# Depthwise convolution of a diffusion backbone on VectorE: one instruction a tap, or two in turn

## The reference, cut to what matters

```
CONV_WIDTH = 31
D_CONV = 512

def dwconv(x, w):
    '''Centred depthwise convolution over positions, zero padded. x (B,T,C), w (W,C).'''
    return lax.conv_general_dilated(x, w[:, None, :], window_strides=(1,), padding='SAME', ...)

def conv_module(glu_in, dw_w, ln_g, ln_b):
    a, b = jnp.split(glu_in, 2, axis=-1)
    u = a * jax.nn.sigmoid(b)
    u = dwconv(u, dw_w)
    u = layer_norm(u, ln_g, ln_b)
    return jax.nn.silu(u)
```

## Time and profile before

| | us |
|---|---|
| median of 3 runs | 1950.89 (1950.55 to 1960.35) |
| span of the profiled execution, first to last instruction | 1948.7 |
| median over that span, what lies around it | 2.2 |
| PE busy | 1757.5 (90%) |
| DVE busy | 1201.7 (62%) |
| POOL busy | 611.3 (31%) |
| ACT busy | 557.4 (29%) |
| share of L1414 in the chain that ended last | 8% |

### The profile page before, as it was taken

One profiled execution on the slowest core, in us unless ns is written; L12 is line 12 of the kernel. 1 busy time (PEld: TensorE's weight loads), 2 busy tenths in 40 slices (PEclk: granted clock), 3 DMA queues, 4 the chain that ended last, 5 costly groups with the idle time before them and its releaser, 6 DMA issues.

```text
span 1948.7 us, 25524 instructions
## 1 busy us (share of the span) xinstructions
PE 1757.5 (90%) x9480; PEld 1495.6 (77%) x9480; DVE 1201.7 (62%) x1757; ACT 557.4 (29%) x777; POOL 611.3 (31%) x282
## 2 busy tenths in 40 slices
PE   5799994777978999999999999798899899999997
PEld 4688883555877888888888888677677778888885
DVE  8888987455877888676853872742683544153243
ACT  1323122553223232122211222231232343223232
POOL 2433330221332343223432323241002245444441
PEclk8699996799988999999999999798899899999998
DMA  8232210002421334333332322031001023332221
GB/s 286 65 80 74 65 44 33 17 17 79 145 80 44 117 100 139 119 96 120 97 119 87 97 86 76 1 111 44 1 1 56 31 87 97 97 98 96 86 92 60
DMA packets 156400, 157.71 MB, mean 81 GB/s; under 512 B 9442, under 2 KB 153506, under 8 KB 156330
## 3 DMA queue, kind: packets, MB, share of 16 engines
q1 hardware_dynamic: 156330, 156.77, 25.1%
HBM read 154.63 MB, written 2.12 MB: 80 GB/s over the span
## 4 chain that ended last, share of the span: by engine, by line
PE 58%; DVE 25%; issue 9%; ACT 3%; DMA 2%; POOL 1%; DVEq 1%; SPq 1%; ACTq 0%; POOLq 0%
PE acc L479 45%; DVE conv_u L1414 8%; DVE ada_acc L1229 4%; PE acc L492 2%; PE acc L822 2%; DVE hid L1585 2%; PE acc L665 2%; DVE xT L1313 2%; DVE ada_acc_b L1229 1%; PE acc L801 1%; PE acc L505 1%; DMA ada_w<-in_ada_w 1%; DVE y L1210 1%; PE acc L776 1%; PE acc L514 1%
## 5 line engine op out<-in xcount | busy, mean ns | idle before, releaser
L1754 POOL TENSOR_TENSOR w_lo<-raw,w_hi 128x1024 fp32r<-128x1024 f32 x190 | 519.7, 2756 | 1033.7 <-ACT w_hi L848 1033.7
L479 PE MATMUL acc<-h_hi,w_hi 128*128 128x512 f32 x1744 | 520.3, 357 | 15.1 <-DVE h_lo L1288 4.4
L479 PE MATMUL acc<-h_lo,w_hi 128*128 128x512 f32 x1744 | 516.4, 355 | 0.0
L479 PE MATMUL acc<-h_hi,w_lo 128*128 128x512 f32 x1744 | 515.7, 355 | 0.0
L479 PEld LDWEIGHTS acc<-h_hi,w_hi 128*128 128x128 f32 x1744 | 287.2, 191 | 66.2 <-DVE h_lo L1288 4.3
L479 PEld LDWEIGHTS acc<-h_lo,w_hi 128*128 128x128 f32 x1744 | 287.0, 191 | 47.2
L479 PEld LDWEIGHTS acc<-h_hi,w_lo 128*128 128x128 f32 x1744 | 286.7, 190 | 47.6
L1229 DVE SCALAR_TENSOR_TENSOR ada_acc<-ada_w,cond,ada_acc 128x256 f32<-128x256 f32 x476 | 278.2, 655 | 1.6
L848 ACT ACTIVATE w_hi<-raw 128x1024 fp32r<-128x1024 f32 x190 | 193.9, 1054 | 219.9 <-PE acc L479 96.8
L1414 DVE SCALAR_TENSOR_TENSOR conv_u<-conv_u,dw_w x120 | 158.5, 1321 | 21.7 <-DVE conv_u L1414 21.0
L479 PE MATMUL acc<-hid_hi,w_hi 128*128 128x512 f32 (+1 forms) x528 | 160.7, 359 | 0.0
(11 more groups left out here) (214 smaller groups left out, 1788.4 us busy)
## 6 DMA issues: line engine op xcount, KB each, us to landing
raw<-in_ffn_w_in SPq DMA_DIRECT2D x88, 512.0 KB, 3.5
ada_w<-in_ada_w SPq DMA_DIRECT2D x80, 512.0 KB, 3.6
raw<-in_ffn_w_out SPq DMA_DIRECT2D x40, 512.0 KB, 3.4
raw<-in_even_w_in SPq DMA_DIRECT2D x24, 512.0 KB, 3.6
ada<-in_ada_w SPq DMA_DIRECT2D x8, 1024.0 KB, 11.8
raw<-in_odd_w_in SPq DMA_DIRECT2D x12, 512.0 KB, 3.4
raw<-in_even_w_out SPq DMA_DIRECT2D x8, 512.0 KB, 4.7
raw<-in_odd_w_out SPq DMA_DIRECT2D x8, 512.0 KB, 3.4
```

The costliest lines, as they stand in the source:

```text
L479: last = nc.tensor.matmul(acc[:, s, m, t0:t1], w[:, slot, kk, c], x[:, k, t0:t1], start=(k == 0 and q == 0), stop=(k == ktiles - 1 and q = ...
L1754: nc.gpsimd.tensor_tensor(w_lo[:, n % 4], raw[:, n % 2], w_hi[:, n % 4].bitcast(F32), ALU.subtract).then_inc(low, 1)
```

## The change

Each tap becomes two instructions, one over the 512 latent columns and one over the 256 context columns, in turn. Each waits for the last instruction but one, which is the one that it adds to; the 15 columns between are no longer computed. Tap 0's two don't wait for each other. The wait for everything before stands once, ahead of a tile's first tap.

```diff
-            taps_len = LAT + HALF + CTX
+            taps = ((HALF, LAT), (U_CTX, CTX))
...
                 with dve.Fori(0, 2) as t:
-                    sd.loop(t, TAPS)
-                    dst = conv_u[:, bass.ds(t + first, 1), HALF:HALF + taps_len]
+                    sd.loop(t, 2 * TAPS)
+                    sd.wait()
                     for w in range(TAPS):
-                        src = conv_u[:, bass.ds(t + (first + 1), 1), w:w + taps_len]
-
-                        sd.wait()
                         tap = dw_w[:, w, bass.ds(t + first, 1)]
-                        if w == 0:
-                            ins = nc.vector.tensor_scalar(dst, src, tap, None, ALU.mult)
-                        else:
-                            ins = nc.vector.scalar_tensor_tensor(dst, src, tap, dst, ALU.mult, ALU.add)
-                        sd.done(ins)
+                        for c, n in taps:
+                            dst = conv_u[:, bass.ds(t + first, 1), c:c + n]
+                            src = conv_u[:, bass.ds(t + (first + 1), 1), c - HALF + w:c - HALF + w + n]
+                            if w == 0:
+                                ins = nc.vector.tensor_scalar(dst, src, tap, None, ALU.mult)
+                            else:
+                                sd.wait(sd.value() - 1)
+                                ins = nc.vector.scalar_tensor_tensor(dst, src, tap, dst, ALU.mult, ALU.add)
+                            sd.done(ins)
                     sd.end(2)
                 sd.wait()
```

## The result

The change makes the kernel about 1% slower: 1970.24 us, the median of 4 runs (1964.3 to 1978.81), beside 1950.72 for the kernel before. The ratio is 1.0096, with a 95% interval of 1.0049 to 1.0143. Forecast were 1996 us. The direction was right and the size was not: 19.5 us came and 45 were forecast. The number that came out is the one of the rival "one window more", 1971.5.

A forecast was written before the change was run, and what follows sets the result against it. DVE's stretch to 329.5 was taken to set L643, PE's 22.1 us behind it. PE's waits for w_lo move L643 from 329.7 to 375, clock terms cancel: 1950.9 + 45 = 1996 us; own range 1982 to 2012, 8 in 10 1935 to 2006.

The forecast's parts named there:

- one window more: Rival, chance 0.24: POOL still gets in at 2.8 us in tiles 1 and 3; L643 at 350, +20.6 us, 1971.5.
- The price of a tap: Convolution on DVE: two overlapping pieces cost 1.06 us a tap against 1.215, 18.6 us saved; added queue work costs nothing.
- POOL's w_lo beside a back-to-back stream: 18 w_lo instructions on the taps cost 2.14 us each back to back against 1.88, 4.7 us lost in all.
- the sum's marker at 315: conv_done, the marker behind the convolution, comes at 315 if w_lo keeps its 5.5 us pairs.
- That POOL is shut out, and that this decides: Convolution: unbroken 32.5 us streams keep POOL from w_lo, PE waits, and L643 starts 45 us later.
- The first pair's wait: Tile 0: the gate unit's w_lo pair, asked for at 138.1, is done at 164.5; PE starts at 162.1.
- POOL gets in during about the first 2.4 us of a back-to-back stream: Beside DVE's streams: POOL enters w_lo during about the first 2.4 us, after that only at a stop.
- POOL asks at about 167.3 ... 2.8 us old: too late: Tile 1: POOL's request misses the stream; w_lo done at 199, PE waits 29 us, qkov 0 is 38.4 us late.
- The clock: L643 may be shorter by 3 us behind busy units, against 3 us for PE's last restart: they cancel.
- POOL as before: Sum if POOL is served as now: -14.2 us, 1937 us, or 1929 if L643 returns to full clock.
- It stays as it was for POOL: Rival, chance 0.27: POOL slips in at piece boundaries even late in a stream, PE isn't delayed; 1937 or 1929 us.
- Nothing gained by overlap: Rival, chance 0.07 with gains that cancel: pieces end to end, 1.03 + 0.2 us a tap, within 2 us of now.

The follow-up runs named there:

- run 4: The changed kernel, with POOL writing zeros by memset to w_lo for the last 20 granules beside the convolution: 1919.52 us, ratio 0.9838.
- run 8: The kernel before, with POOL writing zeros by memset to w_lo for the last 20 granules beside the convolution: 1922.17 us, ratio 0.987.
- run 2: The changed kernel, but at every 4th tap the 512-column piece waits for the last instruction, a stop of DVE: 1939.63 us, ratio 0.9958.
- run 3: The changed kernel, but at every 8th tap the 512-column piece waits for the last instruction, a stop of DVE: 1933.55 us, ratio 0.992.
- run 6: The changed kernel, with a one-column DVE memset (a door) before every 4th tap and no added wait: 1935.18 us, ratio 0.9937.
- run 7: The changed kernel, with one stop of DVE a tile, at tap 16: 1929.11 us, ratio 0.9914.
- run 11: The changed kernel, with a one-column DVE memset (a door) before every 8th tap and no added wait: 1934.6 us, ratio 0.9923.
- run 5: The changed kernel once more, unaltered, to see its spread: 1971.29 us, ratio 1.0103.
- run 9: The changed kernel, but each tap is three pieces of 256 columns, each waiting for the last instruction but two: 2021.41 us, ratio 1.0378.
- run 1: The changed kernel, but the 512-column piece of every tap waits for the last instruction, a stop a tap: 1971.22 us, ratio 1.010.

## Why the prediction was right and where it was wrong

- **The price of a tap: right.** Forecast 1.06 us and nothing for the queue's added work; measured 31.87 us for sixty pieces, and 19.05 us between runs 4 and 8 for 18.9. Every piece of the four tiles started 0.66 or 0.40 us after the one before, where POOL wasn't in between.
- **POOL's w_lo beside a back-to-back stream, 2.14 us instead of 1.88: right.** Four taps with one take 6.47 us against 4.33 in run 2. With POOL served as before, the sum's marker at 315 stands beside 316.85, 315.90 and 315.26 (a stop every 8th tap, a door every 4th and every 8th).
- **That POOL is shut out, and that this decides: right.** Runs 2, 3, 6, 7 and 11 each open the stream now and then, change nothing else, and all are faster than the kernel before.
- **The first pair's wait: right.** Forecast from 138.1 to 164.5, measured 136.92 to 163.34; PE held back until 160.97 (forecast 162.1).
- **The step that failed: "POOL gets in during about the first 2.4 us of a back-to-back stream", and with it "POOL asks at about 167.3 ... 2.8 us old: too late".** POOL asked at 165.84, 2.50 us behind its last entry, and was let in at the boundary 2.85 us behind it. The same came again at 260.30. The prediction measured in time, on an FFN stream that opens with four short tap-0 pieces. Counted, the request that missed there at 964.08 came in the seventh instruction of its stream, where it goes both ways, and the one here in the sixth (fifth, if the piece that had waited for POOL isn't counted). So one pair more got in within tile 1 and one within tile 2, PE was spared the 29 us wait before qkov 0, and L643 began 24.4 us later instead of 45. The trace of before already spoke against an edge of 2.4 us. There POOL asked at 986.23, 3.4 us into a back-to-back stream of DVE's whose first instruction is long, in its sixth instruction, and got in (POOL, then DVE):

```profile
986.23 5.28 POOL L1754 TENSOR_TENSOR w_lo<-raw,w_hi 128x1024 fp32r<-128x1024 f32 x2 [11.36 <-ACT w_hi L848]
```
```profile
982.84 1.76 DVE L1210 TENSOR_TENSOR hid_lo<-hid,hid_hi  x1 [1.73 <-ACT hid_hi L1096]
984.52 0.61 DVE L1222 TENSOR_SCALAR ada_acc<-ada_w,cond 128x256 f32<-128x256 f32 x2
985.04 7.26 DVE L1229 SCALAR_TENSOR_TENSOR ada_acc<-ada_w,cond,ada_acc 128x256 f32<-128x256 f32 x7
```

- **The entry in mid-stream was not foreseen.** POOL had asked at 241.16 and was let in at 252.91, beside the 48th of tile 2's sixty pieces. There the queue's row (REGISTER_ALU) came 0.05 us ahead of its 256-column piece, where it elsewhere comes 0.4 us ahead of one. In run 5 the entry came at the same piece. It spared PE one more wait: the pair was for qkov 4, which began at about 254, and the tile's stream ran until 268.3. Why the queue was late there stays open.
- **The clock was mis-sized.** The forecast set a loss of 3 us against a gain of 3. The three restarts cost 10 us over the units, and L643 behind busy units gave 3.3 back. The 1929 us of "POOL as before" take 8 us for what that bullet puts at 3; run 7, where L643 did follow busy units, saved 4.1 in it, so its 1929.11 doesn't confirm that term.
- **The rival "one window more"** had the waits nearly right (the last before qkov 6, until 301; measured 303.4) and L643 at 350 (measured 354.08), and its 1971.5 us stand beside 1970.24. That the two are so close is in part luck: L643 began 4 us later than it had it and took 3.3 us less, the entry in mid-stream isn't in it, and the profiled execution ended 14.1 us later, not 20. It was given 0.24 where the forecast had 0.42: 0.4 us from an edge that rested on three cases, the two should have been even. The trace of before held five more requests in the eighth instruction of a stream or behind it (at 628.40, 666.35, 702.36, 739.72 and 1110.46, w_lo of 6.1 to 7.5 us), which, beside the one let in at 986.23, would have shown how the edge goes by number.
- **"It stays as it was for POOL" fell** by the rows of 16 to 30 us. By the Trainium skill (SBUF — State Buffer, Who interferes with whom) the two engines exclude each other per instruction. That they don't read at once these traces bear out (6.47 us against 4.33 with one w_lo), but not what the rival drew from it, that POOL's wait ends with the piece that holds it up: 41 boundaries between instructions went by in one wait of POOL's, and 92 in run 9. **"Nothing gained by overlap" fell** too: the Trainium skill (VectorE: DVE Perf Modes, The DRAIN you can't avoid) has it that a semaphore between instructions costs nothing extra, and here, with a semaphore behind every instruction in both, waiting for the last instead of the last but one costs 0.27 us of 1.33 a tap (run 1 against the change).

## What to carry to other kernels

Before a dependent stream on DVE is packed without gaps, look who else waits for the same reads: the gap that looks like waste may be the only moment at which GpSimd gets its turn, and the engine behind GpSimd pays. Pack the stream, but leave an opening every few instructions, by one wait for the last instruction or by one tiny instruction that reads nothing: here one stop in eight taps, at 0.27 us, turned 1% slower into 0.8% faster. And when a forecast hangs on an edge known from three cases, ask whether the edge is one of time or of number, and spread the chances over both sides of it.

## What the runs showed of the hardware that was not expected

- A back-to-back stream of DVE instructions with two inputs keeps a two-input POOL instruction waiting until it stops, with the one exception at 252.91 (and its like in run 5): 23.9 us at 136.92 in the change and 38.5 in run 9, though its instructions start 0.40 or 0.66 us apart.
- Shortly behind a stop or behind POOL's own last turn it is still let in: up to the sixth instruction in every case but one (run 9, 227.12), sometimes in the seventh, and from the eighth on in none of the 80 cases of the FFN's streams. What sets this stays open. The count is a fit; it may be how far DVE's queue has got ahead of its work, which the two exceptions would suit (tap 0's three pieces wait for nothing, and at 252.91 the queue was late), but no run tried that.
- A DVE memset of 0.06 us over one column opens the stream again, at no visible price, and a POOL memset of 128x1024 isn't held up by the stream at all (1.90 us a pair).
- A w_lo instruction costs the stream 2.15 us where pieces overlap (packed, or with a stop behind each tap as in run 1) and 1.88 in single ones with a stop behind each.
